# Nineteen of the 26 expert units that TensorE multiplies while the experts are picked go over to split operands, the high parts made by ScalarE and the low parts by GpSimd

## The chip, the cores and the metric

The kernel runs on one core of one Trainium2 chip. The metric is device time in microseconds. The core's engines are TensorE (PE in the profile; PEld is its weight load), VectorE (DVE), ScalarE (ACT), GpSimd (POOL) and the DMA queue that SyncE (SP) feeds.

## What is computed

256 tokens of width 1024 go through two layers of a first block and one layer of a second. Each layer of the first block mixes (attention, a short convolution, pooling) and then runs a layer of experts chosen per token. The change touches only that expert part:

```
q = (ht @ w_q).reshape(n_tok, PEER_HEADS, PEER_QDIM)
s1 = einsum('thd,kd->thk', q[..., :half], sub_keys[0]); s2 = ... sub_keys[1]
v1, i1 = top_k(s1, 16); v2, i2 = top_k(s2, 16)
top, pos = top_k(v1[..., :, None] + v2[..., None, :] flattened, 16)
eidx = take_along_axis(i1 * 128 + i2, pos); gate = softmax(top)
y = sum over h, k of gate * gelu(ht . expert_u[eidx]) * expert_v[eidx]
```

There are 128 x 128 = 16384 experts and all data is float32. The kernel does not gather experts. It multiplies the tokens with all of expert_u, builds a matrix G of gates (zero where an expert was not picked) and multiplies gelu(products) * G with all of expert_v.

## The kernel before, in words

All weights arrive as a stream of 512 KB units of 128 x 1024 floats. SP puts unit n into slot n % 8 of `RING` as soon as unit n - 8 has been used (`stream`; semaphores `loaded0` to `loaded7` for arrival, `units_used` for use). `RING_LO` is a second view of the same memory, so a low part overwrites its unit.

A unit is multiplied in one of two forms. **Plain**: float32 weights and float32 tokens, one product per 128-column step (L1240). **Split**: the weights are a high part (a copy rounded to fp32r) and a low part (the unit less its high part), the tokens likewise (`H_HI`, `H_LO`), and three products per step, high*high, high*low, low*high (L1243 to L1245). A unit has KD = 8 steps. Elsewhere the high part is made by ScalarE and the low part by VectorE.

The stage in question exists once per layer of the first block. It has these parts.

- The query projection's 16 units, whose top-16 searches VectorE does head by head (`top16`, L1378 to L1384).
- **The picking**: VectorE, with no query work left, joins the two top-16 lists (L1399), searches 256 candidates per row (`top16`), subtracts the maximum (L1403, signals `centred`), and turns positions into expert numbers, twice (L1408 cast, L1409 is_equal, L1412 mult, L1414 reduce, signals `routed`). ScalarE exponentiates the centred scores (L1318, `gate_exp`). TensorE meanwhile multiplies the first units of expert_u ahead: `ahead()` goes over AHEAD = 22 pairs, 44 units. A pair's two products lie in one PSUM bank (6 or 7), pair p waits for the gelu of pair p - 2, and `ahead_gelu(p)` on ScalarE (L1307) takes the pair to `STAGE`, from where SP spills it to DRAM. AHEAD_PICK = 11 pairs, 22 plain units, come before TensorE's transposes of the routes (L1258, behind ScalarE's `by_tile`, L1311).
- **The one-hots**: 64 groups of 4 tokens. VectorE makes one-hot rows (L1426) in one of 3 buffers, GpSimd multiplies half of them by the gates (L1363, signals `gated`), TensorE multiplies them into G (8 matmul records, L1268), ScalarE copies the bank to the arena (L1342). The buffer is free when its G product is made. One more plain unit lies before the first group, and the other 21 units, all split, are spread evenly by step behind the groups (`ahead_by`, `finished`): their high parts by ScalarE (`early_high`, L1335), their low parts by VectorE (L1434).

Every engine executes its list in the order written; nothing reorders it.

Of the kernel before, what the change touches and what calls it, by code (L numbers as in the profile page):

```python
# [22 lines left out]
ALU = mybir.AluOpType  # L23
ACT = mybir.ActivationFunctionType
F32 = mybir.dt.float32
# [9 lines left out]
KD = D // P  # L35
# [5 lines left out]
SLOTS = 8  # L41
# [17 lines left out]


AHEAD = 22
AHEAD_PICK = 11


L_N1, L_N2, L_BADA, L_QG, L_KG, L_CONV, L_PSC, L_SINK = 0, 8, 16, 64, 65, 66, 72, 74
# [87 lines left out]
def program(nc, wstream, consts, mixconst, crow, xT, memT, pos, vec2, s5b, s5c, wglu, wdt, out):  # L153
    ctx = ExitStack()
    with ctx:
# [45 lines left out]
        def S(name):  # L201

            if name not in named:
                named[name] = pools[0][len(named)]
            return named[name]
# [55 lines left out]
        def arrived(eng, u):  # L261

            eng.wait_ge(loaded[u % SLOTS], 16 * (u // SLOTS + 1))

        def used(u):
            return u + 1
# [358 lines left out]
        for layer in range(DEPTH):  # L625
# [530 lines left out]
            STAGE = HOT[:, slot_of[HIGHS - 1], :].rearrange("p (s c) -> p s c", s=2)  # L1156
            kept = 16 * (AHEAD // 2) * layer

            E0 = S_EXP + 2 * AHEAD_PICK + 1
            N_SPLIT = 2 * (AHEAD - AHEAD_PICK) - 1  # L1160
            S0 = N_WQ - PRE

            def ahead_by(g):

                return max(KD * (N_SPLIT - 1) * (g - 2) // (GROUPS - 3), 0)

# [2 lines left out]
                return [n for n in range(N_SPLIT) if g >= 0 and ahead_by(g - 1) < KD * (n + 1) <= ahead_by(g)]  # L1169

            IOTA_BANK = PS[:, 5, 0:P]
            FIRST, FIRST_LO, FIRST_HI = WK[:, 0, 0:512], WK_LO[:, 0, 0:512], WK_LO[:, 0, 512:1024]
            assert S_EXP % 2 == 0

            with nc.Block() as block:
# [22 lines left out]
                @block.tensor  # L1198
                def _(pe):
                    tiles = Tiles()  # L1200
                    tiles.n = PRE

                    def keys(h):

                        pe.wait_ge(S("q_copied"), 2 * h + 2)
                        if h >= 2:
                            pe.wait_ge(S("keys_copied"), h - 1)
                        for m in range(4):
                            tt, half = m // 2, m % 2
                            mm = pe.matmul(PS[:, h % 2, m * P:(m + 1) * P], Q[:, 2 * h + half, tt * P:(tt + 1) * P],  # L1210
                                           PK[:, T + half * P:T + (half + 1) * P], start=True, stop=True)
                        mm.then_inc(S("key_scored"), 1)

                    unit_group(pe, range(S_WQ, S_WQ + PRE), [PS[:, 2 + i, 0:T] for i in range(PRE)], (True,) * PRE)
                    for h in range(1, 8):
                        for i in range(PRE if h == 1 else 2 * h, 2 * h + 2):
                            b = tiles.bank_after(pe, "q_copied")
                            pe.wait_ge(S("split"), i - PRE + 1)
                            unit_product(pe, PS[:, b, 0:T], S_WQ + i, H_HI, H_LO).then_inc(units_used, 1)
                        keys(h - 1)  # L1220
                    keys(7)
                    tiles.n = 0

                    def ahead():

                        for p in range(AHEAD):
                            if p >= 2:
                                pe.wait_ge(S("ahead_gelu"), p - 1)
                            for e in range(2):
                                u = S_EXP + 2 * p + e  # L1230
                                arrived(pe, u)
                                if p + e == 0:
                                    pe.wait_ge(S("h_whole"), KD)
                                dst = PS[:, 6 + p % 2, e * T:(e + 1) * T]
                                if u >= E0:
                                    pe.wait_ge(S("split"), S0 + u - E0 + 1)
                                for k in range(KD):
                                    o = slice(k * P, (k + 1) * P)
                                    if u < E0:
                                        mm = pe.matmul(dst, RING[:, u % SLOTS, o], H32[:, k, :],  # L1240
                                                       start=(k == 0), stop=(k == KD - 1))
                                    else:
                                        pe.matmul(dst, WK_LO[:, u % 2, o], H_HI[:, k, :], start=(k == 0), stop=False)  # L1243
                                        pe.matmul(dst, WK_LO[:, u % 2, o], H_LO[:, k, :], start=False, stop=False)
                                        mm = pe.matmul(dst, RING_LO[:, u % SLOTS, o], H_HI[:, k, :],  # L1245
                                                       start=False, stop=(k == KD - 1))
                                    if k == KD - 1:
                                        mm.then_inc(units_used, 1)
                                    yield

                    first = ahead()
                    for _ in range(2 * KD * AHEAD_PICK):
                        next(first)
                    for i in range(3):
                        pe.wait_ge(S("by_tile"), i + 1)
                        b = tiles.bank(pe)
                        for tt in range(TT):
                            mm = pe.transpose(PS[:, b, tt * P:(tt + 1) * P], PICK[:, i, tt * P:(tt + 1) * P], ident)  # L1258
                        mm.then_inc(S("routes_turned"), 1)

                    for _ in range(KD):
                        next(first)
                    for g in range(GROUPS):
                        pe.wait_ge(S("gated"), g + 1)
                        if g >= 4:
                            pe.wait_ge(S("g_copied"), g - 3)
                        for t in range(4):
                            mm = pe.matmul(PS[:, g % 4, t * P:(t + 1) * P], hots[g % HOTS][:, 0, t, :],  # L1268
                                           hots[g % HOTS][:, 1, t, :], start=True, stop=True)
                        mm.then_inc(S("g_made"), 1)  # L1270
                        for _ in range(ahead_by(g) - (ahead_by(g - 1) if g else 0)):
                            next(first)
                    for _ in first:
                        pass

                @block.scalar
                def _(sc):
# [24 lines left out]
                    def ahead_gelu(p):  # L1302

                        sc.wait_ge(units_used, used(S_EXP + 2 * p + 1))
                        if p >= 2:
                            sc.wait_ge(spilled[p % 2], kept + 16 * (p // 2))
                        act.mark(sc.activation(STAGE[:, p % 2, :], PS[:, 6 + p % 2, :], ACT.Gelu), "ahead_gelu")  # L1307

                    def by_tile(i, src):
# [2 lines left out]
                                               src.rearrange("p (h t k) -> p h t k", h=8, t=TT), ACT.Copy),  # L1312
                                 "by_tile")

                    for p in range(6):
                        ahead_gelu(p)
                    act.wait("centred", 1)
                    act(sc.activation(GT, GT, ACT.Exp), "gate_exp")  # L1318
                    for p in range(6, 9):
                        ahead_gelu(p)  # L1320
                    by_tile(0, SEL[:, 0, :])
                    for p in range(9, AHEAD_PICK):
                        ahead_gelu(p)
                    by_tile(1, SEL[:, 1, :])
                    by_tile(2, GT.rearrange("p a b -> p (a b)"))
                    for i in range(3):
# [9 lines left out]

                    early_high(0)
                    early_high(1)
                    p = AHEAD_PICK
                    for g in range(GROUPS):  # L1340
                        act.wait("g_made", g + 1)
                        act.mark(sc.activation(G[:, :, 4 * g:4 * g + 4],  # L1342
                                               PS[:, g % 4, :].rearrange("p (t i) -> p i t", t=4), ACT.Copy), "g_copied")
                        if KD + ahead_by(g) >= 2 * KD * (p + 1 - AHEAD_PICK):
                            ahead_gelu(p)
                            p += 1
                        for n in finished(g):
                            if n + 2 < N_SPLIT:
                                early_high(n + 2)
                        if g >= GROUPS - PRE:  # L1350
                            split_high(act, S_EXP + V0 + g - (GROUPS - PRE), True)
# [6 lines left out]

                @block.gpsimd
                def _(pool):  # L1360
                    for g in range(GROUPS):
                        pool.wait_ge(S("one_hots"), g + 1)
                        pool.tensor_tensor(hots[g % HOTS][:, 1], hots[g % HOTS][:, 1],  # L1363
                                           J[:, 2, 4 * g:4 * g + 4].unsqueeze(2).to_broadcast([P, 4, P]),
                                           ALU.mult).then_inc(S("gated"), 1)
# [1539 lines left out]
```

## Time and profile before

| | us |
|---|---|
| median of 3 runs (lowest, highest) | 2464.11 (2463.63, 2464.44) |
| the profiled execution's own time | 2463.14 |
| its span, first to last instruction | 2461.3 |
| TensorE busy | 2364.9 (96%) |
| VectorE busy | 1797.1 (73%) |
| ScalarE busy | 1157.5 (47%) |
| GpSimd busy | 148.3 (6%) |

The profile page gives busy time per engine and a line of tenths over 40 slices of the span; further views are a list of instructions in order of time with the idle time before each, groups by line, one line's or tile's instructions with shortest, median and longest duration, and busy time by window with the granted TensorE clock.

### The profile page before, as it was taken

The page shows a single profiled execution, that of the slowest core. Times are in us where ns is not written, and L with a number is a line of the kernel's source. Part 1 is how long each engine was busy: PE and PEld are TensorE (multiplying, and loading weights), DVE is VectorE, ACT ScalarE, POOL GpSimd, SP SyncE. Part 2 cuts the span into 40 slices and gives each one's busy share as a digit, 9 for nine tenths or more (in the row PEclk, how much of TensorE's full clock was granted, in tenths as well). Part 3 has the DMA queues.
Part 4 walks back from the last instruction along what each step waited for, and adds up shares of the span by engine and source line. Part 5 has one row for each costly group of instructions (what it writes and reads, how often), then busy time and mean ns, then how long its engine had stood idle before and what let it go on. Part 6 is the DMA issues. An engine that isn't in the chain of part 4 may idle for free. (4 is left out here: it accounts for less than half of the span.)

```text
span 2461.3 us, 36638 instructions
## 1 busy us (share of the span) xinstructions
PE 2364.9 (96%) x14280; PEld 2123.6 (86%) x14280; DVE 1797.1 (73%) x2913; ACT 1157.5 (47%) x1707; POOL 148.3 (6%) x141
## 2 busy tenths in 40 slices
PE   4979999999999999999999999999999999999998
PEld 4879898888888888889899888888888888898998
DVE  7979997677667676678999676566767576555665
ACT  4542255444545454564135444455545523544554
POOL 0000153000000000000045100000000000000000
PEclk9989999999999999999999999999999999999999
DMA  9365544787676666434544586665555523343553
GB/s 356 134 227 163 157 124 149 267 298 240 233 242 231 239 231 223 148 111 139 177 135 125 188 299 220 204 216 187 189 188 191 191 78 108 124 148 126 189 186 107
DMA packets 133554, 460.63 MB, mean 187 GB/s; under 512 B 15152, under 2 KB 16432, under 8 KB 132912
## 3 DMA queue, kind: packets, MB, share of 16 engines
q1 hardware_dynamic: 133424, 458.90, 55.1%
q8 instruction: 82, 1.34, 0.2%
q14 instruction: 48, 0.39, 0.0%
HBM read 445.73 MB, written 13.11 MB: 186 GB/s over the span
## 5 line engine op out<-in xcount | busy, mean ns | idle before, releaser
L1654 DVE TENSOR_TENSOR ring_lo<-ring,ring_hi 128x1024 fp32r<-128x1024 f32 x421 | 506.9, 1222 | 88.6 <-ACT ring_hi L1557 88.6
L1557 ACT ACTIVATE ring_hi<-ring 128x1024 fp32r<-128x1024 f32 x421 | 435.0, 1054 | 134.0 <-PE banks L346 119.9
L319 PE MATMUL banks<-normed_lo,ring_hi 128*128 128x512 f32 x1344 | 477.9, 398 | 0.0
L344 PE MATMUL banks<-ring_hi,work_lo 128*128 128x512 f32 x1024 | 400.5, 391 | 8.0 <-DVE work_lo L1681 4.3
L345 PE MATMUL banks<-ring_lo,work_lo 128*128 128x512 f32 x1024 | 399.9, 391 | 0.0
L346 PE MATMUL banks<-ring_hi,work_lo 128*128 128x512 f32 x1024 | 399.1, 390 | 0.0
L320 PE MATMUL banks<-normed_lo,ring_lo 128*128 128x256 f32 x1344 | 377.2, 281 | 0.0
L319 PEld LDWEIGHTS banks<-normed_lo,ring_hi 128*128 128x128 f32 x1344 | 252.5, 188 | 61.8
L361 DVE TENSOR_TENSOR ring_lo<-ring,ring_hi 128x1024 fp32r<-128x1024 f32 x185 | 225.0, 1222 | 78.1 <-ACT ring_hi L356 77.5
L320 PEld LDWEIGHTS banks<-normed_lo,ring_lo 128*128 128x128 f32 x1344 | 253.8, 189 | 3.3
L1677 DVE TENSOR_TENSOR work<-banks,work 128x512 f32<-128x512 f32 x84 | 58.1, 692 | 249.2 <-ACT work L1563 249.2
L356 ACT ACTIVATE ring_hi<-ring 128x1024 fp32r<-128x1024 f32 x185 | 194.9, 1055 | 94.9 <-PE banks L311 53.5
L344 PEld LDWEIGHTS banks<-ring_hi,work_lo 128*128 128x128 f32 x1024 | 192.6, 188 | 50.8 <-DVE work_lo L1681 5.2
L346 PEld LDWEIGHTS banks<-ring_hi,work_lo 128*128 128x128 f32 x1024 | 192.6, 188 | 40.9
L1563 ACT ACTIVATE work<-banks 128x512 f32<-128x512 f32 x84 | 50.2, 597 | 372.4 <-PE banks L320 372.4
L345 PEld LDWEIGHTS banks<-ring_lo,work_lo 128*128 128x128 f32 x1024 | 192.6, 188 | 36.9
L309 PE MATMUL banks<-normed_lo,ring_hi 128*128 128x256 f32 x752 | 217.5, 289 | 1.2 <-DVE ring_lo L361 0.8
L310 PE MATMUL banks<-normed_lo,ring_hi 128*128 128x256 f32 x752 | 213.4, 284 | 0.0
L311 PE MATMUL banks<-normed_lo,ring_lo 128*128 128x256 f32 x752 | 213.3, 284 | 0.0
L1363 POOL TENSOR_TENSOR one_hots<-one_hots,routes 128x512 f32<-128x512 f32 x128 | 138.9, 1085 | 579.9 <-DVE one_hots L1426 573.0
L1240 PE MATMUL banks<-work,ring 128*128 128x256 f32 x736 | 159.5, 379 | 0.0
L1240 PEld LDWEIGHTS banks<-work,ring 128*128 128x128 f32 x736 | 139.5, 190 | 18.8
(387 smaller groups left out, 4357.4 us busy)
## 6 DMA issues: line engine op xcount, KB each, us to landing
ring<-wstream SPq DMA_DIRECT2D x716, 512.0 KB, 3.3
arena<-wstream SPq DMA_DIRECT2D x96, 512.0 KB, 5.7
spill<-one_hots SPq DMA_DIRECT2D x44, 256.0 KB, 4.2
rstd<-spill SPq DMA_DIRECT2D x16, 256.0 KB, 4.1
pool_and_keys<-spill SPq DMA_DIRECT2D x14, 256.0 KB, 4.1
routes<-spill SPq DMA_DIRECT2D x14, 256.0 KB, 4.8
residual<-xT SPq DMA_DIRECT2D x1, 1024.0 KB, 7.8
arena<-mixconst SPq DMA_DIRECT2D x2, 512.0 KB, 4.2
```

The source lines that it names most:

```text
L309: pe.matmul(dst, w_hi[:, o], hi[:, k, :], start=(k == 0), stop=False)
L310: pe.matmul(dst, w_hi[:, o], lo[:, k, :], start=False, stop=False)
L311: mm = pe.matmul(dst, w_lo[:, o], hi[:, k, :], start=False, stop=(k == KD - 1))
L319: pe.matmul(dst, w_hi[:, o], HR[:, k, :], start=(k == 0), stop=(k == KD - 1), skip_group_check=True)
L320: mm = pe.matmul(dst[:, 0:T], w_lo[:, o], HR[:, k, 0:T], start=False, stop=(k == KD - 1), skip_group_check=True)
L344: pe.matmul(dst, hi[:, t], w_hi[:, o], start=first, stop=False)
L345: pe.matmul(dst, hi[:, t], w_lo[:, o], start=False, stop=False)
L346: mm = pe.matmul(dst, lo[:, t], w_hi[:, o], start=False, stop=last)
L361: v.mark(v.eng.tensor_tensor(RING_LO[:, u % SLOTS, :], RING[:, u % SLOTS, :], RING_HI[:, u % HIGHS, :].bitcast(F32), ALU.subtract), "split")
L1240: mm = pe.matmul(dst, RING[:, u % SLOTS, o], H32[:, k, :], start=(k == 0), stop=(k == KD - 1))
L1557: sc.activation(RING_HI[:, u % HIGHS, :], RING[:, u % SLOTS, :], ACT.Copy)\
L1654: dve.tensor_tensor(RING_LO[:, u % SLOTS, :], RING[:, u % SLOTS, :], RING_HI[:, u % HIGHS, :].bitcast(F32), ALU.subtract).then_inc(S("spli ...
```

## The change

The number of units before the transposes goes from 22 to PICKED = 26. Of these the 19 in EARLY (numbers 2 to 6, 8 to 17, 19, 21, 23, 25) are multiplied in split form; 0, 1, 7, 18, 20, 22, 24 stay plain. Unit 26, still plain, lies between the transposes and the first group, and 17 units instead of 21 are left for the one-hots. The high part of the m-th early unit is written by ScalarE into one of the three one-hot buffers, which it shares in turn, so from the fourth on it waits until the early unit three before it has been used. GpSimd, idle in the picking before, subtracts to make the low part in place.

```
+PICKED = 26
+EARLY = (2, 3, 4, 5, 6, 8, 9, 10, 11, 12, 13, 14, 15, 16, 17, 19, 21, 23, 25)
...
+                                    if u - S_EXP in EARLY:
+                                        if k == 0:
+                                            pe.wait_ge(S("early_low"), EARLY.index(u - S_EXP) + 1)
+                                        w_hi = early_slot(u)[:, o]
+                                        pe.matmul(dst, w_hi, H_HI[:, k, :], start=(k == 0), stop=False)
+                                        pe.matmul(dst, w_hi, H_LO[:, k, :], start=False, stop=False)
+                                        mm = pe.matmul(dst, RING_LO[:, u % SLOTS, o], H_HI[:, k, :],
+                                                       start=False, stop=(k == KD - 1))
...
-                    for _ in range(2 * KD * AHEAD_PICK):
+                    for _ in range(KD * PICKED):
...
+                    def pooled_high(m):
+
+                        u = S_EXP + EARLY[m]
+                        arrived(sc, u)
+                        if m >= HOTS:
+                            sc.wait_ge(units_used, used(S_EXP + EARLY[m - HOTS]))
+                        act.mark(sc.activation(early_slot(u), RING[:, u % SLOTS, :], ACT.Copy), "pooled_high")
+
+                    def ahead_step(p):
+
+                        for m in range(HOTS, len(EARLY)):
+                            if EARLY[m - HOTS] // 2 == p:
+                                pooled_high(m)
+                        ahead_gelu(p)
+
+                    for m in range(HOTS):
+                        pooled_high(m)
                     for p in range(6):
-                        ahead_gelu(p)
+                        ahead_step(p)
                     act.wait("centred", 1)
                     act(sc.activation(GT, GT, ACT.Exp), "gate_exp")
-                    for p in range(6, 9):
-                        ahead_gelu(p)
+                    for p in range(6, 11):
+                        ahead_step(p)
                     by_tile(0, SEL[:, 0, :])
...
                 @block.gpsimd
                 def _(pool):
+                    for m, n in enumerate(EARLY):
+                        u = S_EXP + n
+                        pool.wait_ge(S("pooled_high"), m + 1)
+                        pool.tensor_tensor(RING_LO[:, u % SLOTS, :], RING[:, u % SLOTS, :], early_slot(u).bitcast(F32),
+                                           ALU.subtract).then_inc(S("early_low"), 1)
```

The first place where the order matters is ScalarE's list around the exponential of the picking, in the first layer. Line numbers of the change are some 14 to 36 higher; L1307 and L1321 are `ahead_gelu`, L1318 and L1349 the exponential, L1335 of the change `pooled_high`. Before:

```order
L1307 ACTIVATE one_hots<-banks 128x512 [waits spilled0,units_used]
L1307 ACTIVATE one_hots<-banks 128x512 [waits spilled1,units_used]
L1318 ACT_TABLE_LOAD
L1318 ACTIVATE arena<-arena 128x256 [waits stage0_17]
L1307 ACT_TABLE_LOAD [waits spilled0,units_used]
```

and with the change:

```order
L1335 ACTIVATE ring_hi<-ring 128x1024 [waits units_used,loaded3]
L1335 ACTIVATE ring_hi<-ring 128x1024 [waits units_used,loaded4]
L1321 ACTIVATE one_hots<-banks 128x512 [waits spilled1,units_used]
L1349 ACT_TABLE_LOAD
L1349 ACTIVATE arena<-arena 128x256 [waits stage0_19]
L1335 ACTIVATE ring_hi<-ring 128x1024 [waits units_used,loaded5,stage0_20]
L1335 ACTIVATE ring_hi<-ring 128x1024 [waits units_used,loaded6]
L1321 ACT_TABLE_LOAD [waits spilled0]
L1321 ACTIVATE one_hots<-banks 128x512 [waits units_used]
```

The two copies ahead of the exponential are the high parts of units 13 and 14, the two behind it those of 15 and 16; `stage0_19` is `centred`, and the first copy behind waits for the exponential's own end too (`stage0_20`).

The second place is GpSimd's list in the same layer, from its branch into the stage on. Before:

```order
L1359 UNCONDITIONAL_BRANCH
L1363 ISA
L1363 TENSOR_TENSOR one_hots<-one_hots,routes 128x512 x64
```

and with the change:

```order
L1390 UNCONDITIONAL_BRANCH
L1395 ISA
L1395 TENSOR_TENSOR ring_lo<-ring,ring_hi 128x1024 [waits stage0_18] x19
L1399 TENSOR_TENSOR one_hots<-one_hots,routes 128x512 [waits stage0_25] x64
```

The 19 subtractions, each behind its high part (`stage0_18`), stand ahead of the 64 gatings.

## Rows read from the trace of the kernel before

**Rows 1.** The page: busy time, GpSimd's busy tenths in 40 slices.
```profile
PE 2364.9 (96%) x14280; PEld 2123.6 (86%) x14280; DVE 1797.1 (73%) x2913; ACT 1157.5 (47%) x1707; POOL 148.3 (6%) x141
...
POOL 0000153000000000000045100000000000000000
```

**Rows 2.** By window, first layer's stage: length, busy us per engine (count), clock, DMA, GB/s.
```profile
212.95:289.00 76.05, 76.05 (x355) 66.91 (x354) 75.05 (x218) 11.14 (x16) 0.00 (x0) 1.00 0.59 182
...
294.10:411.20 117.10, 115.35 (x992) 114.80 (x991) 105.11 (x85) 64.68 (x98) 68.09 (x63) 1.00 0.38 118
```

**Rows 3.** TensorE in order of time, both layers' picking (start, length, [idle before <-releaser]).
```profile
212.95 76.14 PE L1240 MATMUL banks<-work,ring 128*128 128x256 f32 x352
288.93 0.38 PE L1258 MATMUL banks<-consts_sb,arena 128*128 128x128 f32 x2
...
1172.41 76.14 PE L1240 MATMUL banks<-work,ring 128*128 128x256 f32 x352
```

**Rows 4.** TensorE in order of time, a split unit's last step but one and last.
```profile
413.93 0.28 PE L1243 MATMUL banks<-normed_lo,work_lo 128*128 128x256 f32 x1
...
414.17 0.28 PE L1245 MATMUL banks<-normed_lo,ring_lo 128*128 128x256 f32 x1
```

**Rows 5.** TensorE in order of time, group products, three groups apart.
```profile
1284.11 1.05 PE L1268 MATMUL banks<-one_hots 128*128 128x128 f32 x8
...
1289.65 1.05 PE L1268 MATMUL banks<-one_hots 128*128 128x128 f32 x8
```

**Rows 6.** VectorE in order of time through the picking.
```profile
224.86 0.43 DVE L1397 CAST arena<-arena 128x512 f32<-128x512 uint32 x1
225.32 4.43 DVE L1399 TENSOR_TENSOR arena<-arena 128x4096 f32<-128x4096 f32 x1
...
259.68 0.42 DVE L1403 TENSOR_TENSOR arena<-arena 128x256 f32<-128x256 f32 x1
...
261.13 4.43 DVE L1409 TENSOR_TENSOR arena<-arena,consts_sb 128x4096 f32<-128x4096 f32 x1
265.59 4.42 DVE L1412 TENSOR_TENSOR arena<-arena 128x4096 f32<-128x4096 f32 x1
...
289.40 0.29 DVE L1421 COPY banks<-consts_sb 128x128 f32<-128x128 f32 x1
```

**Rows 7.** ScalarE in order of time around the exponential.
```profile
254.59 0.60 ACT L1307 ACTIVATE one_hots<-banks 128x512 f32<-128x512 f32 x1 [6.31 <-PE banks L1240]
...
260.14 0.42 ACT L1318 ACTIVATE arena<-arena 128x256 f32<-128x256 f32 x1 [3.65 <-DVE arena L1403]
```

**Rows 8.** One line's instructions: ns shortest/median/longest, first and last start.
```profile
L1335 ACT ACTIVATE work_lo<-ring x42: 1042/1057/1061, 294.4 to 1366.0; 128x1024 fp32r<-128x1024 f32 x42
```

**Rows 9.** The same of GpSimd's and VectorE's lines in the one-hots.
```profile
L1363 POOL TENSOR_TENSOR one_hots<-one_hots,routes x128: 1040/1042/1997, 292.7 to 1366.4; 128x512 f32<-128x512 f32 x128
...
L1434 DVE TENSOR_TENSOR ring_lo<-ring,work_lo x42: 1215/1466/2116, 296.3 to 1367.1; 128x1024 fp32r<-128x1024 f32 x42
```

**Rows 10.** GpSimd and VectorE in order of time where they meet.
```profile
334.82 1.04 POOL L1363 TENSOR_TENSOR one_hots<-one_hots,routes 128x512 f32<-128x512 f32 x1
334.83 2.12 DVE L1434 TENSOR_TENSOR ring_lo<-ring,work_lo 128x1024 fp32r<-128x1024 f32 x1
336.87 3.47 DVE L1426 TENSOR_TENSOR one_hots<-routes,banks 128x1024 f32<-128x1024 f32 x3
```

**Rows 11.** By window, the first layer's mixing, where TensorE had waited.
```profile
86.00:88.00 2.00, 1.40 (x7) 1.40 (x8) 2.00 (x3) 1.82 (x7) 0.00 (x0) 0.50 0.41 160
88.00:90.00 2.00, 2.00 (x11) 2.00 (x10) 1.93 (x4) 0.95 (x2) 0.00 (x0) 0.50 0.01 2
```

**Rows 12.** TensorE in order of time there: an idle time, then split products.
```profile
82.45 1.10 PE L727 MATMUL banks<-arena 64*128 64x256 f32 x4 [2.39 <-DVE arena L994]
...
88.80 0.41 PE L311 MATMUL banks<-normed_lo,ring_lo 128*128 128x256 f32 x1
89.01 0.41 PE L309 MATMUL banks<-normed_lo,ring_hi 128*128 128x256 f32 x1
...
91.36 0.29 PE L311 MATMUL banks<-normed_lo,ring_lo 128*128 128x256 f32 x1
```

More of the change, by code:

```diff
@@ L61 @@
 AHEAD = 22
-AHEAD_PICK = 11
+PICKED = 26
+EARLY = (2, 3, 4, 5, 6, 8, 9, 10, 11, 12, 13, 14, 15, 16, 17, 19, 21, 23, 25)
 L_N1, L_N2, L_BADA, L_QG, L_KG, L_CONV, L_PSC, L_SINK = 0, 8, 16, 64, 65, 66, 72, 74
@@ L1157, in program @@
             kept = 16 * (AHEAD // 2) * layer
-            E0 = S_EXP + 2 * AHEAD_PICK + 1
-            N_SPLIT = 2 * (AHEAD - AHEAD_PICK) - 1
+            E0 = S_EXP + PICKED + 1
+            N_SPLIT = 2 * AHEAD - PICKED - 1
             S0 = N_WQ - PRE
@@ L1171, in program, with early_slot @@
             IOTA_BANK = PS[:, 5, 0:P]
+            def early_slot(u):
+                return RING_HI[:, slot_of[EARLY.index(u - S_EXP) % HOTS], :]
             FIRST, FIRST_LO, FIRST_HI = WK[:, 0, 0:512], WK_LO[:, 0, 0:512], WK_LO[:, 0, 512:1024]
@@ L1238, in ahead @@
                                     o = slice(k * P, (k + 1) * P)
-                                    if u < E0:
+                                    if u - S_EXP in EARLY:
[6 more added lines that the diff above has]
+                                                       start=False, stop=(k == KD - 1))
+                                    elif u < E0:
                                         mm = pe.matmul(dst, RING[:, u % SLOTS, o], H32[:, k, :],
@@ L1313, in by_tile @@
                                  "by_tile")
+                    def pooled_high(m):
[11 more added lines that the diff above has]
+                        pooled_high(m)
                     for p in range(6):
-                        ahead_gelu(p)
+                        ahead_step(p)
                     act.wait("centred", 1)
                     act(sc.activation(GT, GT, ACT.Exp), "gate_exp")
-                    for p in range(6, 9):
-                        ahead_gelu(p)
+                    for p in range(6, 11):
+                        ahead_step(p)
                     by_tile(0, SEL[:, 0, :])
-                    for p in range(9, AHEAD_PICK):
-                        ahead_gelu(p)
+                    for p in range(11, PICKED // 2):
+                        ahead_step(p)
                     by_tile(1, SEL[:, 1, :])
@@ L1338, in _ @@
                     early_high(1)
-                    p = AHEAD_PICK
+                    p = PICKED // 2
                     for g in range(GROUPS):
@@ L1343, in _ @@
                                                PS[:, g % 4, :].rearrange("p (t i) -> p i t", t=4), ACT.Copy), "g_copied")
-                        if KD + ahead_by(g) >= 2 * KD * (p + 1 - AHEAD_PICK):
+                        if KD * (PICKED + 1) + ahead_by(g) >= 2 * KD * (p + 1):
                             ahead_gelu(p)
```

## The prediction

> **What bounds the kernel now.** I read the page first: TensorE is busy 96% of the span and GpSimd 6%, nearly all of it in two patches [rows 1]. Then the windows of the stage that the change edits: in the picking, 212.95 to 289, TensorE is busy without a gap, and in the one-hots it is busy 115.35 of 117.10 us while VectorE is busy 105.11 [rows 2]. So both parts run at TensorE's pace, GpSimd is free in the picking, and less TensorE work is worth its full time, as long as nothing makes TensorE wait. The second layer runs the same: its first plain unit starts at 1172.41 and the 352 records again take 76.14 us [rows 3]. I work out one layer and double it.
>
> Prices per unit. Plain: 22 units from 212.95 to 288.93, so 3.45 us [rows 3]. Split: products start 0.12 us apart (413.93 to 414.17 is two of them), 24 per unit, 2.88 us [rows 4]. A group's G product: 5.54 us pass between starts three groups apart with one whole split unit (2.88) among them, so 0.89 us each [rows 5].
>
> **The change, part by part.**
>
> (a) TensorE's own work in the picking: 22 x 3.45 = 76.0 becomes 19 x 2.88 + 7 x 3.45 = 78.9, **+2.9**.
>
> (b) One-hots: four split units fewer, 4 x 2.88, **-11.5**. With no wait anywhere a layer would gain 8.6 us, the kernel 17.3.
>
> (c) The new chain. Unit EARLY[m] needs: unit EARLY[m-3] used; ScalarE's copy, 1.06 us [rows 8]; GpSimd's subtraction. Of the latter before has no row: its nearest is the gating of 512 elements, 1.04 us undisturbed [rows 9]. Bounds for 1024 elements: 1.04 if all of it were fixed, 2.5 if the larger op were 20% dearer per element. I take twice the row, 2.08, since it is a streaming op with the same two SBUF operands. The signals between engines cost some 0.1 to 0.2 each. Undisturbed the chain is 3.4 us, and with consecutive early units TensorE has two units (5.8 us) of other work meanwhile: hidden.
>
> (d) Where ScalarE's list stands still. The exponential waits for `centred`. Before, ScalarE was done with pair 5 at 255.2 and sat until VectorE's subtraction at 259.68 let it start at 260.14 [rows 6, 7]. That harmed nobody, as TensorE needed only old gelus. Now the high parts of units 15 and 16 are queued behind it, and the first of them waits for the exponential's end too. TensorE gets there early: units 0 to 14 are 3 plain and 12 split, 10.4 + 34.6 = 45.0, so it is ready for unit 15 at 212.95 + 45.0 = 257.9. Even with no disturbance unit 15 is ready only at 260.14 + 0.42 + 1.06 + 2.08 + some 0.4 of signals = 264.1: a stall of **6.2**.
>
> (e) GpSimd and VectorE get in each other's way. At 334.82 GpSimd starts a gating, VectorE starts the low part of a unit 0.01 later, and that takes 2.12 us instead of 1.22 or so: 1.04 for GpSimd to finish and its own work after it. The one-hot rows that follow, with one operand in PSUM, take 3.47 for three [rows 10]. GpSimd in its turn goes up to 1.997 against 1.04 [rows 9]. So one waits for the whole of the other's instruction when VectorE reads two SBUF tensors. The picking's L1399, L1403, L1409 and L1412 do just that, L1399 once and the last two twice for 4.43 us each [rows 6], and now the subtractions run beside them. Followed through:
>
> - Unit 2 is used at 222.7, the low part of unit 5 runs 224.0 to 226.1. VectorE's cast (L1397), due at 224.86, I let wait for it as well (a one-input op; if it doesn't wait, L1399 does): VectorE is 1.2 late, L1399 runs 226.6 to 231.0. The low part of unit 6 waits out that instruction and is ready at 233.1, TensorE at 231.4: stall **1.8**. TensorE comes to unit 15 at 259.7.
> - `centred` comes at 261.4, the high part of unit 15 at 262.8. L1409 started at 262.3, so GpSimd gets in at 266.8 and is ready at 268.9: stall **9.3** instead of the 6.2 of (d).
> - L1412 has waited since 266.8 and now runs to 273.3. Unit 16's low part follows, to 275.4. TensorE would be through with unit 15 at 271.9: stall **3.7**.
> - Then reduces and the freed chain let GpSimd run ahead, and TensorE finds units 17 to 25 ready. The two 4.43 us instructions of the second round hold up single low parts, which have plain units between them.
>
> (f) TensorE's clock. In the first layer's mixing TensorE waited 2.39 us and more in small pieces, and the granted clock then stood at 0.50, which is the 1.2 GHz level; split products started 0.21 us apart (88.80 to 89.01) against 0.12, until a little after 91 [rows 11, 12]. So after 9.3 idle us I expect unit 15 at 24 x 0.213 = 5.1 us, hidden in the stall before unit 16, and unit 16 at 5.1 too: **+2.2**. Bounds: 0 (the clock holds) and 4.5 (two units pay in the open).
>
> TensorE then reaches the transposes at 212.95 + 78.9 + 1.8 + 9.3 + 3.7 + 2.2 = 308.8 against 288.9. VectorE, whose chain ended at 289.7 [rows 6], is delayed about 9 us by GpSimd, to 299, and doesn't bound.
>
> (g) Waits in the one-hots. With three buffers, group g + 3 needs VectorE's rows (3.47 / 3, some 1.13), the gating (1.04) and signals, 2.5 us, after group g's product. TensorE's own work in between is now 4.0 us (three groups at 0.89 and 2.1 steps of 0.36 behind each, less one product), before 4.7. A low part on VectorE (median 1.47, at most 2.12 [rows 9]) then fits the slack of 1.5 only just, where 2.1 was ample. 17 such parts x 0.25 = **+4**; bounds 0 and 17 x 0.6 = 10.
>
> Sum per layer: 2.9 - 11.5 + 1.8 + 9.3 + 3.7 + 2.2 + 4 = **+12.4**, twice that **+24.8**. Against the profiled execution's own 2463.14 that is 2487.9. It lies 1.0 below the median of the runs, so 2464.11 + 24.8 = **2489**. All else is as it was: the spills follow the gelus as before, and weights have the slack of a slower TensorE.
>
> Two rules of the Trainium skill bear on (c) and (e). GPSIMD Engine Reference (elementwise accounting) gives 4497 ns for a float32 tensor_tensor of 2048; an estimate from it is 2.25 us for 1024, and the sum would be +0.7 per layer more. SBUF - State Buffer (Who interferes with whom) says that a VectorE op with two SBUF inputs and a GpSimd op that reads SBUF exclude each other for the whole instruction and that issue order decides; by that rule, the trace agrees (2.12 us). It adds that a reduce or another one-input op outside the two-port modes never contends; no row of before can show that for top-16 searches, as GpSimd was idle then, and if they did wait too, VectorE's chain would grow, at most by 19 x 2.08.
>
> **Rivals.**
>
> **A, VectorE keeps the port between its own instructions** (0.2). Then unit 15's low part gets in only when L1414 starts, at 271.3, ready 273.4: stall 13.8 instead of 9.3 + 3.7, and a further 3.4 at unit 19 from the second round, 4.2 more per layer: 2497. For it: L1409 and L1412 follow one another within 0.03 us [rows 6]. Against it: each waits for a semaphore in between.
>
> **B, no exclusion in the picking** (0.13). Then only (d) is left: 2.9 - 11.5 + 6.2 + 1 (clock) + 0.5 = -0.9 per layer, 2462, within the noise. [Rows 10] speak against it.
>
> **C, faster: TensorE hides the delay** (0.05). The deciding point is the sum of all new waits per layer: under 8.6 us the change wins. It takes that GpSimd's op costs near 1.04 (the lower bound), no exclusion, the clock holding: stall 5.1, 2.9 - 11.5 + 5.1 = -3.5 per layer, 2457. It can't get to the full -17.3, because ScalarE's list holds unit 15 back whatever GpSimd does.
>
> The rest, my forecast, has 0.62. That the change doesn't do what it says is ruled out by the order of the instructions.
>
> **Numbers.** 0.2% (4.9 us) is about what a measurement of this kernel can tell. Faster 0.07 (C and the lower edge of B), same 0.11, slower 0.82. At the low end (f), (g) and the stall at unit 16 fall away, 2.2 + 4 + 3.7 = 9.9 per layer, 2469, and I go 2 further towards B: 2467. At the high end stands rival A with half of the upper bound of (g) on top, 3 per layer: 2503.
>
> **What would show it.** In the changed profile: TensorE idle 9 us near 260 (again near 1219) before a split unit, released by GpSimd, a clock near 0.5 just behind it; GpSimd's subtractions at 2.1 with a few of 6 us; L1409 or L1412 at 6.5 instead of 4.43; transposes near 309. I am wrong if unit 15 starts before 262, if L1412 stays at 4.43 beside a subtraction, or if the one-hots part shrinks by more than 11 us.

## The result and the profile after

The change makes the kernel slower: 2491.37 us (median of 5 runs, 2486.95 to 2494.46) against 2464.11, a ratio of 1.0108 (95% interval 1.0095 to 1.0122). The profiled execution took 2486.95 us, span 2485.2, against 2463.14 and 2461.3.

The page of the changed kernel, busy time and GpSimd's slices:

```profile
PE 2361.4 (95%) x14520; PEld 2126.9 (86%) x14520; DVE 1798.5 (72%) x2905; ACT 1187.1 (48%) x1737; POOL 276.9 (11%) x179
...
POOL 0003664000000000000665200000000000000000
```

TensorE's busy time falls by only 3.5 us [rows 1] although 30 more units are multiplied in the cheaper form, and the span grows by 23.9: the time is in waits, and in units that run at a lower clock. By window (length, busy us of PE, PEld, DVE, ACT, POOL, clock, DMA share, GB/s), the picking and the one-hots of the first layer:

```profile
214.02:309.00 94.98, 83.51 (x572) 79.83 (x570) 83.42 (x219) 31.80 (x39) 65.36 (x19) 0.93 0.55 174
...
313.30:423.70 110.40, 105.80 (x890) 102.92 (x889) 97.42 (x80) 58.82 (x90) 67.03 (x63) 1.00 0.32 101
```

Before, TensorE was busy without a gap in the first and for 115.35 of 117.10 us in the second [rows 2]. In the picking TensorE is now idle for 11.5 us and its clock is at 0.93. TensorE in order of time shows where, in the first layer (start, length, idle before and releaser):

```profile
214.02 7.07 PE L1254 MATMUL banks<-work,ring 128*128 128x256 f32 x32
...
234.71 0.55 PE L1249 MATMUL banks<-normed_lo,ring_hi 128*128 128x256 f32 x1 [2.12 <-POOL ring_lo L1395]
...
238.96 0.28 PE L1251 MATMUL banks<-normed_lo,ring_lo 128*128 128x256 f32 x1
...
270.49 0.55 PE L1249 MATMUL banks<-normed_lo,ring_hi 128*128 128x256 f32 x1 [7.65 <-POOL ring_lo L1395]
...
277.00 0.35 PE L1249 MATMUL banks<-normed_lo,ring_hi 128*128 128x256 f32 x1 [1.21 <-POOL ring_lo L1395]
...
279.94 0.28 PE L1249 MATMUL banks<-normed_lo,ring_hi 128*128 128x256 f32 x1
...
308.12 0.38 PE L1272 MATMUL banks<-consts_sb,arena 128*128 128x128 f32 x2
```

The lines with a wait are the starts of units 6, 15 and 16, all released by a low part of GpSimd; 238.96 is the last product of unit 6 and 279.94 the start of unit 17. From the first plain product to the transposes it is 308.12 - 214.02 = 94.10 us; before, 75.98 [rows 3]. From the transposes to the first product of the next stage (429.51, L345) it is 121.39; before, 416.31 (L344) - 288.93 = 127.38. The stage as a whole goes from 203.36 to 215.49, **+12.13**, and in the second layer from 203.33 to 215.45, +12.12. Both layers together are 24.25; the two profiled executions differ by 23.81. The medians differ by 27.3, since the profiled execution is the fastest of the five; the 3 us beyond the stage are of the size of the scatter described below.

VectorE in order of time through the picking:

```profile
225.92 1.96 DVE L1433 CAST arena<-arena 128x512 f32<-128x512 uint32 x1
227.91 4.43 DVE L1435 TENSOR_TENSOR arena<-arena 128x4096 f32<-128x4096 f32 x1
...
262.28 0.43 DVE L1439 TENSOR_TENSOR arena<-arena 128x256 f32<-128x256 f32 x1
...
263.72 4.42 DVE L1445 TENSOR_TENSOR arena<-arena,consts_sb 128x4096 f32<-128x4096 f32 x1
268.18 6.45 DVE L1448 TENSOR_TENSOR arena<-arena 128x4096 f32<-128x4096 f32 x1
...
279.44 6.51 DVE L1445 TENSOR_TENSOR arena<-arena,consts_sb 128x4096 f32<-128x4096 f32 x1
285.99 6.50 DVE L1448 TENSOR_TENSOR arena<-arena 128x4096 f32<-128x4096 f32 x1
```

In [rows 6] the cast takes 0.43 and the long instructions 4.43. Now the cast (L1433) takes 1.96, and of the four long ones behind the searches (L1445 and L1448, twice) the first keeps its 4.42 and the other three take 6.45, 6.51 and 6.50: each waits out a subtraction of GpSimd. Between L1435's end and L1439, where VectorE searches, 29.94 us pass, 29.93 before, though GpSimd worked on eight subtractions beside them: the searches don't wait.

GpSimd's two lines (ns shortest, median, longest), and in order of time the subtraction of unit 15:

```profile
L1395 POOL TENSOR_TENSOR ring_lo<-ring,ring_hi x38: 2349/2400/6587, 215.8 to 1266.5; 128x1024 fp32r<-128x1024 f32 x38
```
```profile
L1399 POOL TENSOR_TENSOR one_hots<-one_hots,routes x128: 1038/1040/1955, 311.8 to 1392.0; 128x512 f32<-128x512 f32 x128
```
```profile
264.32 6.02 POOL L1395 TENSOR_TENSOR ring_lo<-ring,ring_hi 128x1024 fp32r<-128x1024 f32 x1 [6.48 <-ACT ring_hi L1335]
```

It could start at 264.32, behind the exponential and its own high part, and finished at 270.34, where an undisturbed one takes 2.40: L1445 ran until 268.14 and kept GpSimd out that long. L1448 in its turn, started at 268.18, had to wait until 270.34 and then took the usual 4.3. This exclusion in both directions is what "the port" stands for below. ScalarE, in order of time around the exponential:

```profile
255.27 0.58 ACT L1321 ACTIVATE one_hots<-banks 128x512 f32<-128x512 f32 x1
255.87 1.28 ACT L1349 ACT_TABLE_LOAD   x1
262.74 0.42 ACT L1349 ACTIVATE arena<-arena 128x256 f32<-128x256 f32 x1 [5.59 <-DVE arena L1439]
263.19 2.00 ACT L1335 ACTIVATE ring_hi<-ring 128x1024 fp32r<-128x1024 f32 x2
```

For 5.59 us it stands at the exponential with two copies behind it that it could have made.

The clock, by window in the long wait and behind it:

```profile
266.00:268.00 2.00, 0.00 (x0) 0.00 (x0) 2.00 (x1) 1.99 (x3) 2.00 (x1) 0.50 0.00 0
...
272.00:274.00 2.00, 2.00 (x11) 2.00 (x11) 2.00 (x1) 0.00 (x0) 2.00 (x1) 0.50 0.00 0
274.00:276.00 2.00, 1.79 (x10) 1.59 (x8) 1.97 (x2) 0.11 (x1) 2.00 (x1) 0.63 0.00 0
276.00:278.00 2.00, 1.00 (x8) 1.03 (x9) 2.00 (x1) 1.44 (x2) 2.00 (x2) 1.00 0.57 125
```

The clock fell while TensorE waited. Unit 15 (270.49 to 275.79) ran at 0.50, the 1.2 GHz level; unit 16, from 277.00 on, was back at 2.4 GHz.

**How runs are compared.** The unchanged code behind the second layer's stage took 1085.6 us in the profiled execution of before, 1084.0 in that of the change and 1094.0 in that of one experiment (e3), with a mean clock of 0.99, 0.99 and 0.98. In e2, e4 and e5 it took 1093.6 to 1094.1 too, in e8 1090.0. Whole times therefore scatter by up to 10 us for reasons outside the edit, and the experiments are read by the stage itself, which repeats within 0.15 us between the layers (but for e7, whose layers differ by 2.5).

### The profile page after: what moved, and what is told of

The parts are those of the page before. It is cut to its first block and busy times, and to the rows that moved or that the text cites. A ratio compares the mean times of both kernels' runs of the same rounds, so it can differ in the third digit from the quotient of the medians.

```text
span 2485.2 us, 37222 instructions
## 1 busy us (share of the span) xinstructions
PE 2361.4 (95%) x14520; PEld 2126.9 (86%) x14520; DVE 1798.5 (72%) x2905; ACT 1187.1 (48%) x1737; POOL 276.9 (11%) x179
## 5 line engine op out<-in xcount | busy, mean ns | idle before, releaser
L345 PE MATMUL banks<-ring_hi,work_lo 128*128 128x512 f32 x1024 | 400.5, 391 | 6.7 <-PEq L1181 3.7
L345 PEld LDWEIGHTS banks<-ring_hi,work_lo 128*128 128x128 f32 x1024 | 192.6, 188 | 49.4 <-issue 4.0
L1395 POOL TENSOR_TENSOR ring_lo<-ring,ring_hi 128x1024 fp32r<-128x1024 f32 x38 | 130.7, 3459 | 363.9 <-ACT ring_hi L1335 363.9
L1462 DVE TENSOR_TENSOR one_hots<-routes,banks 128x1024 f32<-128x1024 f32 x128 | 150.2, 1213 | 29.0 <-ACT routes L1359 24.2
```

Source lines behind the costliest of these rows:

```text
L345: pe.matmul(dst, hi[:, t], w_hi[:, o], start=first, stop=False)
```

## The experiments

"Picking" is from the first plain product to the first transpose, "one-hots" from there to the next stage's first product, both in the first layer. Each ratio is to executions of the unchanged kernel taken beside that experiment, whose medians were 2463.32 (e1, e2, e3, e5), 2463.81 (e4, e6, e7) and 2462.28 (e8). e2, e5 and e6 leave low parts out of the result: they price a step and are no kernels to use.

| kernel | picking | one-hots | stage | median us | ratio to before (95%) |
|---|---|---|---|---|---|
| before | 75.98 | 127.38 | 203.36 | 2464.11 | |
| the change | 94.10 | 121.39 | 215.49 | 2491.37 | 1.0108 (1.0095 to 1.0122) |
| e1, exponential later | 82.68 | 124.82 | 207.50 | 2473.66 | 1.0047 (1.0029 to 1.0065) |
| e2, GpSimd fills zeros | 86.55 | 121.39 | 207.94 | 2476.58 | 1.0046 (1.0027 to 1.0065) |
| e3, move alone | 89.79 | 121.40 | 211.19 | 2486.91 | 1.0088 (1.0063 to 1.0114) |
| e5, e1 and e2 together | 78.84 | 121.40 | 200.24 | 2459.36 | 0.9981 (0.9966 to 0.9996) |
| e6, e3 with VectorE filling zeros | 89.79 | 117.02 | 206.81 | 2468.61 | 1.0023 (1.0010 to 1.0035) |
| e4, 24 units, 14 split | 75.12 | 128.84 | 203.96 | 2468.85 | 1.0016 (1.0005 to 1.0027) |
| e7, 24 units, 13 split | 75.37 | 127.98 | 203.35 | 2461.47 | 0.9992 (0.9977 to 1.0006) |
| e8, 24 units, 11 split | 76.53 | 124.75 | 201.28 | 2457.19 | 0.9981 (0.9971 to 0.9991) |

### e1: the exponential two pairs later

```
-                    for p in range(6):
+                    for p in range(8):
                         ahead_step(p)
...
-                    for p in range(6, 11):
+                    for p in range(8, 11):
```

> The change, but ScalarE's exponential stands behind pair 7 instead of behind pair 5, so the high parts of units 15 to 19 no longer queue behind it. Theory (order and port together): the 7.7 us wait before unit 15 and its cold clock go, GpSimd and VectorE still block each other; the picking falls from 94.1 to about 83 to 88 us per layer, but VectorE's delayed chain then shows before the last transposes; 5 to 7 us less per layer, 2477 to 2481. Rival (order alone, the port costs nothing): the picking falls to about 79, some 12 less per layer, 2467. Rival (port alone, the order doesn't matter): no difference, 2487 to 2491.

The wait before unit 15 is gone; what is left in the picking is the wait before unit 6 (2.11 us, and some 1.6 for the lower clock behind it). The stage is 8.0 us shorter than the change's, more than the 5 to 7 expected, and 2473.66 lies below the 2477 to 2481 expected. It is not the whole 15: the picking gives 11.4, but the one-hots take 3.4 more, as TensorE now comes to the transposes ahead of VectorE. TensorE in order of time:

```profile
297.28 0.44 PE L1272 MATMUL banks<-consts_sb,arena 128*128 128x128 f32 x2 [1.80 <-ACT arena L1325]
298.48 0.69 PE L1272 MATMUL banks<-consts_sb,arena 128*128 128x128 f32 x2 [0.76 <-ACT arena L1325]
298.96 4.91 PE L1254 MATMUL banks<-work,ring 128*128 128x256 f32 x16
```

The plain unit behind takes 4.91 instead of 3.62: the clock fell again. "The order alone" would have given a picking of 79, "the port alone" no difference; both rivals are ruled out.

### e2: GpSimd writes zeros

```
-                        pool.tensor_tensor(RING_LO[:, u % SLOTS, :], RING[:, u % SLOTS, :], early_slot(u).bitcast(F32),
-                                           ALU.subtract).then_inc(S("early_low"), 1)
+                        pool.memset(RING_LO[:, u % SLOTS, :].bitcast(F32), 0.0).then_inc(S("early_low"), 1)
```

> The change, but GpSimd fills the low part of each early unit with zeros instead of subtracting: the low parts of 19 units per layer are left out of the result; the order of every engine is the same, and GpSimd no longer reads SBUF in the picking. Theory (order and port): VectorE's 4.43 us instructions stay at 4.43, the wait before unit 6 and the one before unit 16 go, the one before unit 15 stays at about 5 us with the clock's cost on top; picking 94.1 to about 87, so 7 to 8 us less per layer, 2472 to 2476. Rival (port alone): all waits go, the picking is 79 and the kernel near 2461. Rival (order alone): only GpSimd's shorter instruction shows, about 1.5 us per layer, 2486.

The fill reads nothing and is never held up, though two of them (261.83 to 263.73) run beside L1444. VectorE's four long instructions are back at their old length. GpSimd's line (ns shortest, median, longest) and, from VectorE's order of time:

```profile
L1395 POOL MEMSET ring_lo<- x38: 951/952/957, 214.8 to 1247.9; 128x1024 f32 x38
```
```profile
261.25 4.43 DVE L1444 TENSOR_TENSOR arena<-arena,consts_sb 128x4096 f32<-128x4096 f32 x1
265.72 4.42 DVE L1447 TENSOR_TENSOR arena<-arena 128x4096 f32<-128x4096 f32 x1
```

and TensorE has a single wait in the picking, the one for ScalarE's order:

```profile
262.93 0.55 PE L1249 MATMUL banks<-normed_lo,ring_hi 128*128 128x256 f32 x1 [4.86 <-POOL ring_lo L1395]
```

86.55 is TensorE's own 78.87, that wait, and 2.8 for some six microseconds at half clock behind it. So of the change's 15.2 us of delay in the picking, 7.6 are GpSimd's length and the port; the rest is there without them. The length alone would add some 1.5 to the wait before unit 15 (an estimate, 2.40 less 0.95), so most of the 7.6 is the port.

### e3: only the four units move

```
-EARLY = (2, 3, 4, 5, 6, 8, 9, 10, 11, 12, 13, 14, 15, 16, 17, 19, 21, 23, 25)
+EARLY = ()
...
-                    for m in range(HOTS):
+                    for m in range(min(HOTS, len(EARLY))):
                         pooled_high(m)
```

> 26 plain units in the picking, none split: the move of four units out of the one-hots alone. GpSimd does nothing in the picking. By TensorE's work alone a layer changes by 26 x 3.45 - 76.0 - 11.5 = +2.2 us, 2468.5. Theory: the one-hots with 17 low parts are as in the change, 121.4 from the transposes on against 127.4 before (6 less rather than 11.5), so +13.8 - 6.0 = +7.8 per layer, 2479 to 2480. Rival (the extra waits in the one-hots come from something that the early split form leaves behind, not from fewer units): the one-hots give 11.5, 2468 to 2469.

Picking 89.79 and one-hots 121.40, the latter as in the change to 0.01: the waits in the one-hots come with the move of the four units, not with what was split in the picking. The stage is 7.8 longer than before's, as expected. The time as a whole was not: 2486.91 instead of 2479 to 2480. In the profiled execution the untouched end of the kernel took 1094.0 us, 8.4 more than in before's.

### e5: both

The two edits of e1 and e2 in one kernel.

> Both edits at once: exponential behind pair 7 and GpSimd filling zeros (low parts of 19 units per layer left out of the result). Theory: TensorE finds every unit ready, the picking is 79 us, the rest as in the change, 15 us less per layer than the change, 2460 to 2462. If something else than the order and the port held the picking up, it stays above 82.

78.84 us, TensorE's own work (78.87) with no wait left. The order of ScalarE's list and GpSimd's subtraction (its length and the port) are the whole of the picking's delay.

### e6: the one-hots' low parts without reading

e3, and:

```
-                                v.mark(dve.tensor_tensor(RING_LO[:, u % SLOTS, :], RING[:, u % SLOTS, :],
-                                                         WK_LO[:, u % 2, :].bitcast(F32), ALU.subtract), "split")
+                                v.mark(dve.memset(RING_LO[:, u % SLOTS, :].bitcast(F32), 0.0), "split")
```

> The move alone (26 plain units), and in the one-hots VectorE fills the low parts of the 17 split units with zeros instead of subtracting: these low parts are left out of the result. Theory (the extra waits there are VectorE's low part plus GpSimd's gating that shuts it out, eating the slack of three buffers): from the transposes on 121.4 falls to 113 to 116.5, picking unchanged at 89.8. Rival (the waits come from ScalarE's copies or from TensorE's own order): it stays at 121.

VectorE's fill is 0.912 us, and the one-hots fall from 121.40 to 117.02, 0.5 above the expected span but far from the rival's 121. Who TensorE waited for in the one-hots (us in total, times, longest): before (288 to 417), in e3 and in e6 (300 to 425):

```profile
PE banks L1268 <- POOL one_hots L1363: 1.8, 2, 1.4
```
```profile
PE banks L1282 <- POOL one_hots L1399: 4.6, 11, 1.4
```
```profile
PE banks L1282 <- POOL one_hots L1399: 1.6, 6, 0.4
```

With the fill the waits are back at before's level. So VectorE's low part, lengthened where GpSimd's gating shuts it out, makes 4.4 of the 5.5 us that the one-hots fall short of TensorE's saving. How that divides between the length and the port was not tried, nor what the fill would give with before's 21 units.

### e4 and e7: 24 units

e4:

```
-PICKED = 26
-EARLY = (2, 3, 4, 5, 6, 8, 9, 10, 11, 12, 13, 14, 15, 16, 17, 19, 21, 23, 25)
+PICKED = 24
+EARLY = (3, 4, 5, 6, 7, 8, 9, 10, 11, 12, 16, 17, 21, 23)
...
-                    for p in range(6):
+                    for p in range(7):
...
-                    for p in range(6, 11):
+                    for p in range(7, 10):
```

> A version made to beat both: 24 units in the picking, 14 of them split (3 to 12, 16, 17, 21, 23), the exponential behind pair 6, the first routes' copy behind pair 9. By the same walk through the rows, with GpSimd's subtraction at 2.35 us and the exclusion, every low part is ready in time and VectorE's chain ends when TensorE does. Theory: picking 75 to 76 us per layer (76.0 before), from the transposes on 123 to 124 (127.4 before), 4.3 less per layer than before, ratio about 0.9965. Rival (any GpSimd work beside VectorE's picking costs more than it brings): the picking is above 80 and the kernel no faster than before.

e7, the same with EARLY = (3, 5, 7, 8, 9, 10, 11, 12, 13, 16, 19, 20, 23) and the ranges (8) and (8, 9):

> A second version: 24 units, 13 of them split (3, 5, 7 to 13, 16, 19, 20, 23), the exponential behind pair 7, the first routes' copy behind pair 8. Theory: within 1 us per layer of the first version, picking 75 to 77, ratio about 0.9965. Rival: as for the first version.

The pickings are as forecast, 75.12 and 75.37. The rest was missed, and so were the ratios (0.9965 expected): e4's one-hots are 128.84, longer than before's with two units fewer. TensorE is now too early. In order of time and by window, e4:

```profile
289.54 0.44 PE L1272 MATMUL banks<-consts_sb,arena 128*128 128x128 f32 x2 [2.40 <-ACT arena L1325]
290.74 0.69 PE L1272 MATMUL banks<-consts_sb,arena 128*128 128x128 f32 x2 [0.76 <-ACT arena L1325]
291.22 4.98 PE L1254 MATMUL banks<-work,ring 128*128 128x256 f32 x16
```
```profile
290.00:293.00 3.00, 2.26 (x7) 0.59 0.28 107
293.00:296.00 3.00, 3.00 (x13) 0.84 0.02 5
```

One subtraction of GpSimd had held a cast of VectorE (2.46 instead of 0.29), so its chain ended later than TensorE, which waited 2.40 and 0.76 us and then ran at the lower level: the mean granted clock is 0.59 over 290 to 293. e7 shows how much is wait and how much clock. Its first layer has one-hots of 127.98, its second 125.45 with the same order. VectorE in both, then TensorE:

```profile
260.88 1.85 DVE L1439 TENSOR_TENSOR arena<-arena 128x256 f32<-128x256 f32 x1
...
1220.74 1.07 DVE L1439 TENSOR_TENSOR arena<-arena 128x256 f32<-128x256 f32 x1
```
```profile
291.29 0.44 PE L1272 MATMUL banks<-consts_sb,arena 128*128 128x128 f32 x2 [1.41 <-ACT arena L1325]
292.49 0.44 PE L1272 MATMUL banks<-consts_sb,arena 128*128 128x128 f32 x2 [0.76 <-ACT arena L1325]
292.77 5.31 PE L1254 MATMUL banks<-work,ring 128*128 128x256 f32 x16
...
1250.55 0.44 PE L1272 MATMUL banks<-consts_sb,arena 128*128 128x128 f32 x2 [0.77 <-ACT arena L1325]
1251.58 0.44 PE L1272 MATMUL banks<-consts_sb,arena 128*128 128x128 f32 x2 [0.59 <-ACT arena L1325]
1251.85 3.62 PE L1254 MATMUL banks<-work,ring 128*128 128x256 f32 x16
```

In the first layer a subtraction held VectorE's L1439 up for longer, TensorE waited 2.17 us instead of 1.36, and the clock fell; in the second it did not. Of the 2.5 us between the layers 0.8 is wait and 1.7 (5.31 less 3.62) is clock.

### e8: eleven units, none in VectorE's way

e7 with EARLY = (3, 5, 7, 8, 9, 10, 11, 12, 13, 16, 19) and the ranges (8) and (8, 10).

> 24 units in the picking, only 11 of them split (3, 5, 7 to 13, 16, 19), the exponential behind pair 7, so placed that every subtraction of GpSimd falls beside VectorE's searches and none holds VectorE up, and TensorE reaches the transposes just behind VectorE's chain instead of ahead of it. Theory: picking 76.5 us, the gap before the transposes 0.8 as before and no fall of the clock there, from the transposes on 124 to 125 (127.4 before), 201 to 201.5 in all against 203.35 before, in both layers; 4 us less in all, ratio about 0.998. Rival (TensorE's clock falls at the transposes whatever the length of the wait): from the transposes on 128 as in the first version, no gain.

76.53, 124.75 and 201.28, in the second layer 76.53, 124.73 and 201.26. VectorE's instructions keep their length, and TensorE comes to the transposes with the old gap and full clock:

```profile
263.25 4.43 DVE L1445 TENSOR_TENSOR arena<-arena,consts_sb 128x4096 f32<-128x4096 f32 x1
267.70 4.42 DVE L1448 TENSOR_TENSOR arena<-arena 128x4096 f32<-128x4096 f32 x1
```
```profile
292.74 0.74 PE L1272 MATMUL banks<-consts_sb,arena 128*128 128x128 f32 x4 [0.78 <-ACT arena L1325]
293.32 3.62 PE L1254 MATMUL banks<-work,ring 128*128 128x256 f32 x16
```

2.1 us less than before per layer, ratio 0.9981 (0.9971 to 0.9991): it beats both kernels, by a little. As whole times go that is near the limit of what can be told; the stage shows it in both layers. Only e7's second layer, where the picking takes 75.38 and the clock holds all the same, is shorter still: 200.82.

## Why the prediction was right

2489 was forecast, 2491.4 measured, and per layer +12.4 against +12.13. By its steps, first layer:

- **(a)** 78.9 for TensorE's own work: e5 shows 78.84. Right.
- **(b), (g)** -11.5 and +4: together -7.5, measured -5.99. One of the two terms that were mis-sized is (g): 5.5 instead of 4, inside its bounds (0 to 10). Its mechanism stands by e3 and e6. The other is (f).
- **(c)** A subtraction is 2.40 us, not 2.08; the row of half the size was doubled, and 13% were missing. The estimate from the Trainium skill's GPSIMD Engine Reference (elementwise accounting), 2.25, was nearer and still short.
- **(d)** ScalarE's list holds back unit 15. Right, by e1 and by the 4.86 us that remain in e2. The predicted 6.2 had the longer subtraction in it; less the 1.13 that the fill saves on 2.08, it is 5.1.
- **(e)** The waits before units 6, 15 and 16 were put at 1.8, 9.3 and 3.7 and are 2.12, 7.65 and 1.21. All three are there, at the places named, and the instructions of 4.43 us are at 6.5 as foretold. VectorE's cast did wait for GpSimd. The idle time is 11.0 instead of 14.8, since TensorE arrived later: units 6 and 15 ran at a lower clock, which turned idle time into slow time. The delay that stands at unit 16's start is as forecast: 277.00 - 214.02 less 47.8 of TensorE's own work (3 plain and 13 split units) is 15.2, against 14.8. VectorE's chain ended at 298.5, forecast 299. By the Trainium skill's SBUF - State Buffer (Who interferes with whom), a VectorE instruction with one SBUF input, outside the two-port modes, doesn't contend; no row of before could show it for the searches, and the trace of the change agrees (29.94 us of searches against 29.93).
- **(f)** The +2.2 did not come. Unit 15 ran cold, as foretold, 5.3 us instead of 2.9, inside the delay of (e); but unit 16 ran at full clock (279.94 - 277.00 = 2.94). Unit 6 ran cold in part (238.96 + 0.12 - 234.71 = 4.4 instead of 2.9), which was not foretold and cost nothing here: TensorE came that much later to unit 15, which was not ready until 270.34. In e1, where no wait follows, it shows in full.

That the sum came within 0.3 us is luck in part. The picking's delay as a whole, 15.2, was forecast at 17.0; it came 1.8 short, and (g) 1.5 over, so the two misses nearly cancel.

Rival A (VectorE keeps the port between its instructions) falls: GpSimd got in between L1445 and L1448, the subtraction of unit 15 ending at 270.34 and not behind L1448. B and C needed L1448 at 4.43, and it took 6.45; C needed a subtraction near 1.04 too, and it took 2.40.

## What to carry to other kernels

A helper engine that was idle is not free: ask what it shares (here it and VectorE shut each other out) and which instructions of the other engine are long enough to hold it. When an in-order engine gets a new producer's work, look for the old wait in its list that used to be harmless; everything queued behind it inherits that wait. And the engine that sets the pace gains from becoming faster only up to the next engine's chain: in e8 it comes just behind that chain, in e4 and in e7's first layer ahead of it, and against e8 being ahead cost more in the one-hots (4.1 and 3.2 us) than it saved in the picking (1.4 and 1.2).

## What the runs showed that was not expected

- Waits of some two microseconds already brought the clock down: 2.12 before unit 6 in the change did. In e4 waits of 2.40 and 0.76 us at the transposes were followed by a window at 0.59, and the plain unit behind took 4.98 us instead of 3.62; 1.41 and 0.76 in e7's first layer made it 5.31. With 0.77 and 0.59 (e7's second layer), 0.78 (e8) and 0.77 (before) nothing fell, nor behind a single wait of 1.35 in before's one-hots (at 298.52).
- The untouched last stretch of the kernel took 1084.0 us in one profile and 1094.0 in another, at a mean clock of 0.987 and 0.978. An estimate from these: against full clock the one lost 0.013 x 1084.0 = 14 us and the other 0.022 x 1094.0 = 24, so the clock makes the whole difference. What brings it down there more often was not found.
